# Attention over pairs of heads: outputs feature-major in column halves, the division ahead of the turn, scores four items ahead

## The reference, cut to what matters

```python
# layer 0: 8 heads of 64; latent queries see latent keys (with a bias) and context keys,
# context queries see context keys only
s_loc = einsum('bhrqd,bhrjkd->bhrqjk', qg, kg) * scale + bias
s_ctx = einsum('bhrqd,bhld->bhrql', qg, k_ctx) * scale
p_loc, p_ctx = joint_softmax([s_loc, s_ctx])        # exp(s - max) / sum, over both together
o = p_loc @ vg + p_ctx @ v_ctx
# layer 1, window_gqa: 8 query heads, 2 key heads, a sink logit per head in the softmax
# layer 1, diff_attend: 4 heads with two maps each
a = p[:, :, 0] - lam * p[:, :, 1]
o = a @ v                                            # v is 128 wide; then an RMS norm over 128
```

## Time and profile before

| what | value |
|---|---|
| median of three runs | 2750.54 us |
| the profiled execution | 2752.89 us |
| its span | 2751.1 us |
| TensorE busy | 2641.9 us, 96% of the span |
| VectorE busy | 1401.4 us, 51% |
| ScalarE busy | 571.7 us, 21% |
| GpSimd busy | 545.3 us, 20% |
| chain that ended last, share of TensorE | 89% |
| even attention stage | 1602.49 to 1662.71 us |
| odd attention stage | 2249.17 to 2328.02 us |

### The profile page before, as it was taken

How to read it: one execution, slowest core, us unless ns; L and a number is a source line. 1 busy time by engine, 2 the same in 40 slices (tenths; PEclk the granted TensorE clock), 3 DMA queues, 4 the chain that set the end, 5 groups by cost and what they waited for, 6 DMA issues and landing times.

```text
span 2751.1 us, 38407 instructions
## 1 busy us (share of the span) xinstructions
PE 2641.9 (96%) x15510; PEld 1859.8 (68%) x15510; DVE 1401.4 (51%) x2718; ACT 571.7 (21%) x1142; POOL 545.3 (20%) x420
## 2 busy tenths in 40 slices
PE   7999999999999999999999999999999998999998
PEld 4347568888865655789964464788888756655554
DVE  2556366466758677533556542765555335410111
ACT  1215221100033334322022041100000225201110
POOL 0000034444400000047830000444454000000000
PEclk8999999999999999999999999999999998999998
DMA  8551035555333423445445400554543300499995
GB/s 299 199 185 53 31 124 199 182 179 175 110 86 99 115 74 100 152 151 179 144 128 208 145 31 32 177 188 163 168 142 113 124 1 1 171 417 412 415 404 219
DMA packets 218210, 446.71 MB, mean 162 GB/s; under 512 B 18762, under 2 KB 115849, under 8 KB 214955
## 3 DMA queue, kind: packets, MB, share of 16 engines
q1 hardware_dynamic: 176688, 329.78, 33.4%
q10 hardware_dynamic: 41338, 114.40, 12.3%
HBM read 443.01 MB, written 1.13 MB: 161 GB/s over the span
## 4 chain that ended last, share of the span: by engine, by line
PE 89%; DVE 5%; ACT 2%; DMA 1%; issue 1%; POOL 0%; SPq 0%; DVEq 0%; ACTq 0%; POOLq 0%
PE bank L1101 34%; PE bank L929 24%; PE bank L2955 5%; PE bank L953 4%; PE bank L945 3%; PE bank L2974 3%; PE bank_pair L2955 2%; PE bank L2464 1%; DMA slot<-in_ada_w 1%; PE bank L2991 1%; PE bank L2040 1%; PE bank_pair L2974 1%; PE bank L2033 1%; PE bank L2457 1%; PE bank L2928 1%
## 5 line engine op out<-in xcount | busy, mean ns | idle before, releaser
L1101 PE MATMUL bank<-arena,slot 128*128 128x256 f32 (+1 forms) x3704 | 677.0, 343 | 6.3 <-DVE arena L1081 2.9
L1101 PEld LDWEIGHTS bank<-arena,slot 128*128 128x128 f32 x3704 | 605.0, 191 | 70.5 <-issue 8.0
L1114 POOL TENSOR_TENSOR slot<-slot 128x512 f32<-128x512 f32 (+3 forms) x208 | 269.3, 1295 | 1578.5 <-PE bank L1101 699.6
L929 PE MATMUL bank<-uT,slot 128*128 128x512 f32 (+2 forms) x1312 | 484.8, 525 | 2.8 <-ACT arena L2073 2.8
L929 PEld LDWEIGHTS bank<-uT,slot 128*128 128x128 f32 (+1 forms) x1312 | 246.5, 190 | 217.2 <-issue 205.0
L1101 PE MATMUL bank<-uT,slot 128*128 128x256 f32 (+1 forms) x1728 | 335.4, 351 | 6.3 <-ACT uT L681 6.1
L1101 PEld LDWEIGHTS bank<-uT,slot 128*128 128x128 f32 x1728 | 290.7, 192 | 44.6 <-ACT uT L681 10.4
L1115 POOL TENSOR_TENSOR slot<-slot 128x512 f32<-128x512 f32 (+3 forms) x208 | 286.8, 1379 | 0.0
L929 PE MATMUL bank<-arena,slot 128*128 128x256 f32 (+1 forms) x576 | 185.2, 485 | 3.8 <-DVE arena L1762 2.3
L929 PEld LDWEIGHTS bank<-arena,slot 128*128 128x128 f32 x576 | 111.9, 195 | 75.8 <-issue 66.9
L650 DVE SCALAR_TENSOR_TENSOR arena<-arena 128x1024 f32<-128x1024 f32 x95 | 122.3, 1297 | 11.9 <-issue 8.8
(11 more groups left out here) (459 smaller groups left out, 3064.9 us busy)
## 6 DMA issues: line engine op xcount, KB each, us to landing
slot<-in_ffn_w SPq DMA_DIRECT2D x42, 2048.0 KB, 8.7
arena<-in_ada_wt ACTq DMA_DIRECT2D x100, 512.0 KB, 3.6
slot<-in_moe_w SPq DMA_DIRECT2D x62, 704.0 KB, 16.8
arena<-in_moe_w SPq DMA_DIRECT2D x52, 704.0 KB, 17.8
rstd<-in_ada_wt ACTq DMA_DIRECT2D x48, 512.0 KB, 3.6
slot<-in_moe_w SPq DMA_DIRECT2D x11, 2048.0 KB, 18.8
slot<-in_ssd_w_in SPq DMA_DIRECT2D x32, 512.0 KB, 6.9
uT<-in_ada_wt ACTq DMA_DIRECT2D x28, 512.0 KB, 3.6
```

Of the source, the lines that this page charges most:

```text
L929: ins = pe.matmul(bank[0:m, 0:t1 - t0], w[:, k, c0:c0 + m], x[:, k, t0:t1], start=(k == 0), stop=(k == kt - 1))
L1101: ins = pe.matmul(bank[:, u * n:u * n + n], a[:, k, u * P:u * P + P], x[:, k, :], start=(k == 0), stop=(k == self.h - 1))
L1114: pool.tensor_tensor(out[:, :, 0:c], x[:, :, 0:c], y[:, :, 0:c], op)
```

## The change

It touches only `Attention` and the two functions that list its items. Items with one map (all of the even stage, the first 16 of the odd stage) are now handled in pairs throughout:

- **o of a pair** is one result. The values of each head (128 keys x 64) are stationary and the turned probabilities (128 keys x 128 queries) move. The first head's output goes to partitions 0 to 63 of a bank, the second's to 64 to 127 (`outputs_pe`). The result has features on partitions, and DVE copies it straight to `m_y`. The turn f and its copy are dropped for these items.
- **The division** is done on the probabilities before they are turned: DVE computes the reciprocal and scales the 128 x 512 or 128 x 256 tile in SBUF in place (`normalise`). t waits for this.
- **Scores four items ahead** instead of two. In step n DVE does max(n+4), normalise(n+3) and, when n is even, the copy of the pair that ended with n-1. ACT does exp(n+4) before turned(n), where it had turned first.
- The probabilities have six buffers and the turned ones four.

Diff items keep their operations, the turn f and their two items ahead.

TensorE, in the middle of the even stage, before: t and o alternate item by item, o with 64 moving columns.

```diff
         m_s = [[uT[:, 2 * i + j, :] for j in range(2)] for i in range(2)]
-        m_pt = [uT[:, 4 + i, :] for i in range(2)]
+        m_ps = [uT[:, i, :] for i in range(4)] + [m_o[:, 0:512], m_o[:, 1024:1536]]
+        m_pt = [uT[:, 4 + i, :] for i in range(4)]
...
-            def __init__(self, items, turns, ahead):
-                self.items, self.turns, self.ahead = items, turns, ahead
+            AHEAD = {1: 4, 2: 2}
+
+            def __init__(self, items, turns):
+                self.items, self.turns, self.steps = items, turns, range(-self.AHEAD[1], len(items) + 2)
                 self.maps = list(itertools.accumulate(len(it["maps"]) for it in items))
                 N, order = len(items), []
-                for n in range(-ahead, N + 2):
-                    for m in self.scored(n + ahead):
+                for n in self.steps:
+                    for m in self.scored(n):
                         order += [("s", m, j) for j in range(len(items[m]["maps"]))]
                     if 0 <= n < N:
                         order += [("t", n, 0)]
-                    if 0 <= n - 1 < N:
+                    if 0 <= n - 1 < N and not (self.paired(n - 1) and n % 2):
                         order += [("o", n - 1, 0)]
                     if n - 2 in turns:
                         order += [("f", n - 2, 0)]
...
+            def due(self, n):
+
+                for maps, ahead in self.AHEAD.items():
+                    m = n + ahead
+                    if 0 <= m < len(self.items) and self.paired(m) == (maps == 1):
+                        yield m
+
             def scored(self, n):
 
-                if n >= len(self.items):
-                    return []
-                return [n] if not self.paired(n) else [] if n % 2 else [n, n + 1]
+                for m in self.due(n):
+                    if not self.paired(m):
+                        yield m
+                    elif m % 2 == 0:
+                        yield from (m, m + 1)
...
+            def outputs_pe(self, pe, B, n):
+
+                its = self.items[n - 1:n + 1]
+                bank = B.empty(pe, self.order["o", n, 0])
+                for m in (n - 1, n):
+                    B.freed(pe, self.order["t", m, 0])
+                last = len(its[0]["v"]) - 1
+                for t in range(last + 1):
+                    for a, it in enumerate(its):
+                        ins = pe.matmul(bank[64 * a:64 * a + 64, 0:P], it["v"][t], m_pt[(n - 1 + a) % 4][:, t * P:t * P + P],
+                                        start=(t == 0), stop=(t == last))
+                ins.then_inc(B.full_sem, 1)
+
             def score(self, n, j):
-                return m_s[n % 2][j][:, 0:self.items[n]["nk"]]
+                tile = m_ps[n % 6] if self.paired(n) else m_s[n % 2][j]
+                return tile[:, 0:self.items[n]["nk"]]
+
+            def made(self, n):
+
+                return "o", n + (self.paired(n) and n % 2 == 0), 0
+
+            def normalise(self, dve, ch, pr, n):
+
+                it, (den, es, rc) = self.items[n], self.stats(n, 0)[2:5]
+                dve.wait_ge(*pr)
+                if it["sink"] is not None:
+                    dve_link(ch, dve.tensor_tensor(den, den, es, ALU.add))
+                dve_link(ch, dve.reciprocal(rc, den))
+                s = self.score(n, 0)
+                dve.tensor_scalar(s, s, rc, None, ALU.mult).then_inc(*S("pn").given())
...
                     elif kind == "t":
-                        two = len(it["maps"]) == 2
-                        pe.wait_ge(*S("pn" if two else "pr").taken("pe"))
-                        S("pr").passed("pe", 2 if two else 0)
+                        pe.wait_ge(*S("pn").taken("pe"))
                         bank = B.empty(pe, i)
                         for t in range(nk // P):
                             ins = pe.transpose(bank[:, t * P:t * P + P], self.score(n, 0)[:, t * P:t * P + P], ident)
                         ins.then_inc(B.full_sem, 1)
+                    elif kind == "o" and self.paired(n):
+                        self.outputs_pe(pe, B, n)
...
+            def turned(self, act, B, n):
+
+                i, nk = self.order["t", n, 0], self.items[n]["nk"]
+                if n >= 4:
+                    B.full(act, self.order[self.made(n - 4)])
+                bank = B.full(act, i)
+                act.activation(m_pt[n % 4][:, 0:nk], bank[:, 0:nk], ACT.Copy).then_inc(*B.free(i))
+
             def act(self, act, B, ch):
                 N = len(self.items)
-                for n in range(-self.ahead, N + 1):
+                for n in self.steps:
+                    due = list(self.due(n))
+                    for m in due:
+                        if self.paired(m):
+                            self.probabilities(act, B, m)
                     if 0 <= n < N:
-                        i, nk = self.order["t", n, 0], self.items[n]["nk"]
-                        if n >= 2:
-                            B.full(act, self.order["o", n - 2, 0])
-                        bank = B.full(act, i)
-                        act.activation(m_pt[n % 2][:, 0:nk], bank[:, 0:nk], ACT.Copy).then_inc(*B.free(i))
-                    if n + self.ahead < N:
...
+                        self.turned(act, B, n)
+                    for m in due:
+                        if not self.paired(m):
+                            self.probabilities(act, B, m)
...
-                    if 0 <= n - 1 < N:
+                for n in self.steps:
+                    due = list(self.due(n))
+                    for m in due:
+                        for j in range(len(self.items[m]["maps"])):
+                            self.maximum(dve, ch, B, m, j)
+                    for m in self.due(n - 1):
+                        if self.paired(m):
+                            self.normalise(dve, ch, (pr, before + self.maps[m]), m)
+                    for m in due:
+                        if not self.paired(m):
+                            self.combine(dve, ch, (pr, before + self.maps[m]), m)
+                    if ("o", n - 1, 0) in self.order:
                         it, i = self.items[n - 1], self.order["o", n - 1, 0]
-                        den, es, rc = self.stats(n - 1, 0)[2:5]
-                        w = it["v"][0].shape[1]
+                        bank = B.full(dve, i)
                         if it["sub"]:
                             dve.wait_ge(*S("root").taken("dve"))
-                            rc = self.stats(n - 1, 1)[5]
+                            dve.tensor_scalar(it["o"], bank[:, 0:P], self.stats(n - 1, 1)[5], None, ALU.mult)\
+                               .then_inc(*B.free(i))
                         else:
-                            dve.wait_ge(pr, before + self.maps[n - 1])
-                            if it["sink"] is not None:
-                                dve_link(ch, dve.tensor_tensor(den, den, es, ALU.add))
-                            dve_link(ch, dve.reciprocal(rc, den))
-                        bank = B.full(dve, i)
-                        dve.tensor_scalar(it["o"], bank[:, 0:w], rc, None, ALU.mult).then_inc(*B.free(i))
+                            dve.tensor_copy(it["o"], bank[:, 0:P]).then_inc(*B.free(i))
...
-            rows = m_o.rearrange("p (t c) -> p t c", t=4)
-            items, turns = [], {}
+            items = []
...
-                        o=rows[:, t, h * 64:h * 64 + 64]))
-                if t == 3:
-                    n = len(items)
-                    turns[n - 1] = (m_y[:, 4 + f, :], [rows[:, t, f * P:f * P + P] for t in range(4)], None, range(n - 8, n))
-            return items, turns
+                        o=m_y[:, 4 + f, t * P:t * P + P]))
+            return items, {}
```

More of the change, by code:

```diff
@@ L2474, in pe, with probabilities @@
                         ins.then_inc(B.full_sem, 1)
+            def probabilities(self, act, B, m):
+                it = self.items[m]
+                for j in range(len(it["maps"])):
+                    mx, nm, den, es = self.stats(m, j)[0:4]
+                    i = self.order["s", m, j]
+                    act.wait_ge(*S("nm").taken("act"))
+                    if it["sink"] is not None:
+                        act.activation(es, sinks[:, it["sink"]:it["sink"] + 1], ACT.Exp, bias=nm)
+                    act.activation(self.score(m, j), B[i][:, 0:it["nk"]], ACT.Exp, scale=0.125, bias=nm,
+                                   accum_out=den).then_inc(*B.free(i))
+                    act.drain().then_inc(*S("pr").given())
@@ L2583, in odd_attention @@
                         v=[m_v[:, j, 64 * (h // 4):64 * (h // 4) + 64] for j in range(4)],
[L2584 to L2587 removed]
+                        o=m_y[:, f, t * P:t * P + P]))
             for d, t in itertools.product(range(4), range(2)):
```

64 lines of the change are left out of this document (22 added, 42 removed).

## The result

| | before | after |
|---|---|---|
| median | 2752.45 us (12 runs) | 2757.69 us (12 runs) |
| ratio, 95% interval | | 1.0019 [1.0011, 1.0026] |
| the profiled execution, its span | 2752.89, 2751.1 us | 2755.91, 2754.1 us |
| TensorE busy | 2641.9 us | 2629.5 us |
| VectorE busy | 1401.4 us | 1410.5 us |

The change is a loss of about 5 us (0.11 to 0.26%), at the edge of what a measurement tells from none. TensorE has 12 us less to do and the program ends no earlier. The forecast was 2751.5 us, 1.0 us above the 2750.54 that before had then.

The account below looks back on a forecast made before the run. TensorE's work bounds the even stage before, a ring across engines after; even stage +1.7, odd stage -1.8, clock +1.1 sum to +1.0 us, median 2750.54 to 2751.5 us; own range 2747 to 2756, 80% range 2742 to 2759.

Parts of the forecast that it names:

- Rival 2: Pauses ahead of the first o in both stages: clock stays low 8 us, costing 8 us in all; 2758.4 us, chance 0.17.
- a ring: One-map pairs: o, copy, next pair's second maximum, its exp, turned copy, next o; even-stage period 14.30 us against 14.27.
- C1: First of four steps in an even-stage period: next o at 3.71 us, TensorE alone at 3.64.
- L2: Fourth step of an even-stage period: o possible at 13.94 us, TensorE by its own work 14.30; next o 14.30.
- TensorE's own work per period: Even stage, four pairs: scores, t and o together 11.7 us instead of 14.27, about 2.5 us relieved.
- C2: Second step of an even-stage period: next o at 7.37 us, TensorE had work to 5.6 only; about 1.5 us waiting.
- L1: Third step of an even-stage period: next o at 10.44 us, with about 1.5 us of waiting.
- o of an L pair 1.02: TensorE: sixteen records take 1.02 us to the next start, 1.12 with entering the form, against 1.88 before.
- Rival 3: Column halves don't overlap when moving data differ, so o is longer in both stages: +13 us, 2763.5 us, chance 0.05.
- The fills: Starts of the attention stages: first o after 10.8 us in the even and 12.7 us in the odd stage.
- The clock: Granted clock falling behind the fills: +1.1 us for the odd stage, nothing for the even one.
- Rival 1: TensorE stays the bound: even stage gains 4 x 2.5 less 1, odd stage 1.8; 2739.7 us, chance 0.14.

Follow-up runs that it names:

- E1: The changed kernel with ACT doing turned(n) ahead of exp(n+4); median 2743.44 us, ratio 0.9969 to the kernel before.
- E2: The changed kernel with DVE copying a pair's output one step later; median 2750.06 us, ratio 0.9992 to the kernel before.
- E7: The changed kernel with a pair's output matmuls issued head after head instead of in turn; 2762.39 us in one run.
- E4: The changed kernel without scaling the probabilities by the reciprocal, so weights aren't normalised; 2748.3 us in one run.
- E3: The changed kernel with twelve identity matmuls ahead of the first o of each attention stage; median 2753.52 us, ratio 1.0012 to the kernel before.
- E8: E1 with six identity matmuls ahead of the first o of each attention stage; median 2741.67 us, ratio 0.9961 to the kernel before.
- E10: E8 with DVE dividing item n+3 before the maximum of item n+4; median 2777.43 us, ratio 1.0095 to the kernel before.
- E6: E1 with one-map items scored two ahead instead of four; median 2749.08 us, ratio 0.9993 to the kernel before.

## Why the prediction was right, and where not

- **The number: inside the wide range, and not by the right size.** +1.0 us was forecast and +5.2 measured, with an interval of 3.0 to 7.2 that leaves +1.0 out. Rival 2 (2758.4) lies nearer to 2757.69 than the forecast does (2751.5). Its sign, a granted clock under 0.9 over the first 20 us of a stage, just failed to show (0.91 in both stages), and the clock was down for about 5 us, not 8.
- **The bound moves from TensorE to a ring: right, by trace and by E1.** Period 14.30 forecast, 14.31 measured; steps 3.71, 3.66, 3.07, 3.86 against 3.73, 3.66, 3.02, 3.90. In steps C1 and L2 TensorE sets the step (the forecast had the ring just ahead of it in C1), in the other two the wait ahead of o does.
- **TensorE's own work per period: too low.** 11.7 us was summed up, and the waits put at about 1.5 us in each of C2 and L1. The period less its waits is 14.31 - 1.42 - 0.55 = 12.34, with 12.28 busy in E1: the sum left out what lies between neighbouring operations, as the turn behind an o, 0.58 us in L1 (1627.87 to 1628.45) for the 0.44 taken. So TensorE was relieved of 1.9 us a period, not 2.5. The period came right all the same because TensorE sets it in C1 and L2 only, where the steps were priced within 0.1.
- **What is in the ring: right in the order, too narrow for C2.** E2 took the copy out of the ring and step C2 lost only 0.15 us. The forecast had DVE's max and division ahead of the copy in that step; it is they, with exp ahead of turned, that hold it.
- **o of an L pair 1.02: right** (1.02; the sum of TensorE's work took 1.12). Rival 3 falls. Head after head costs 0.5 us per L pair, not 0.86, and nothing per C pair (E7): its price was too high, if that order stands for no overlap.
- **The division 0.64: right** (0.157 and 0.487 in the groups). The scaling is worth 0.33 us per period (E4).
- **The fills: right.** 10.8 and 12.7 forecast, 10.75 and 12.90 measured.
- **Even stage +1.7, odd -1.8, both without the clock: nearly right.** E3, whose clock doesn't fall behind the fills, has +2.00 and -2.07. The even stage of after, 63.37 us, is just outside the 61 to 63 that was named.
- **The clock: the term that was mis-sized.** +1.1 was taken, half of the odd stage's worst and nothing for the even stage; E3 measures 1.15 + 1.67 = 2.8. The even stage's wait was forecast well, 2.5 us for 2.43, and taken as too short for a fall: it sufficed, and 1.53 did in E1. The odd stage's wait was put at 3.8 us and was 2.74. It is rival 2's mechanism at a third of its price.
- **The sum.** Stages: +3.15 - 0.40 = +2.75, and the two profiled executions differ by 3.02. That these agree is chance: the untouched parts ahead of, between and behind the stages differ by +1.38, +1.70 and -2.83. Over all eleven profiled executions these parts take 1599.7 to 1604.6, 586.5 to 589.8 and 419.3 to 423.1 us, with nothing changed in them. The medians of 12 runs differ by 5.2. The stages of one execution leave 2.5 us of it without an account: after's profiled execution is the fastest of its twelve, 1.8 below its median, and before's lies 0.4 above its own. Part of the scatter goes with the clock: its mean over an execution of after is 0.983 in the fastest (2755.91 us) and 0.980 in the two slowest (2760.55 and 2762.41).
- **Rival 1, TensorE stays bound,** isn't the case of the change as it stands. With the ring cut and the clock kept (E8) the attention stages give back 4.8 and 6.8 us, together 11.5, and the kernel goes to 0.9961. The rival had 10.8, but as 9 and 1.8: the near match of the totals is luck. Its even stage was too good because TensorE's work was summed too low.

The Trainium skill (TensorEngine Tiling, PSUM Bottleneck) says that tiling speeds up TensorE but not the emptying of PSUM, and that after a fourfold speedup the copy out of PSUM may become the bottleneck; the prediction put it more firmly. The trace agrees that o waits for ACT's copy out of a bank. Yet ACT is busy 9.07 of 14.31 us there, and E1 mends it with the same copies in another order; more copying capacity wasn't what was lacking.

## What to carry to other kernels

When an engine is relieved, walk the loop that the engines' fixed orders make, hop by hop, before counting the gain: three engines below 90% busy can still be bound by one ring, and here swapping two instructions on the one with the least work of the three turned a loss of 5 us into a gain of 8. Ahead of a wait, issue first what another engine stands still for, then what is needed steps later; but put nothing that waits for a fresh result ahead of the work that would cover that wait (E10). A longer lookahead has its price in the fill, and the fill's pause can cost again as much in clock behind it. A stage's length in one execution can hold or lack a fall of the clock of 1.4 to 1.7 us: compare step by step before a difference is put down to an edit.

## What the runs showed of the hardware

- Behind the fills the granted clock fell with a pause of TensorE of 2.43 us ahead of the first o (after, even), 2.74 (after, odd), 1.53 (E1, even), each of the even ones with one of 0.72 us three or four us earlier, and with two of 1.02 and 0.98 us with 0.66 us of work between them (E6, odd). It stayed up with 1.11 us (E1, odd), 1.83 (E4, odd), 0.59 and 0.72 (E6, even) and 0.72 and 0.19 (E8, even).
- The length of one pause doesn't decide it: with 2.74 us ahead of the first o of the odd stage the clock fell in after and E7 and stayed up in E2. With 2.91 us ahead of the first f of the diff items it fell in after (0.50 over 2314.34 to 2319.00) and stayed up in E1, E3, E4 and E8. What decides is open.
- In the stretches behind the fills it was 0.66 to 0.75 in the mean over 5 or 6 us, a mix of the two levels, 1.2 and 2.4 GHz. One fall cost 1.15 to 1.7 us of a stage. Matmuls of the identity in the pause of the even stage went with a clock that stayed up (E3, E8) and made the first o at most 0.2 us later.
- The column halves of one float32 output, with different heads' data moving, take 1.02 us for sixteen records when issued in turn. Head after head, sixteen take 1.51, but eight take 0.58 to 0.59 in either order; why eight don't suffer stays open, and with it whether overlap is the whole reason.
